# Attention summed by parts: value differences instead of weights, and future keys set to one on GpSimd

## The chip, the cores and the metric

The kernel runs on one core of a Trainium2 chip. The metric is the device time of one execution in microseconds (us); for the kernel before, three executions were timed, and one more was recorded by the profiler.

## The reference, cut to what matters

The program computes a state-space layer with an MLP, then a "stick-breaking" attention layer with an MLP, then a second block (a recurrent mixer, a sparse attention and a feed-forward part). Sequence length is 512, width 1024. Only the stick-breaking attention is touched: 16 heads of 64, for each query t and key s < t

```
z_ts   = q_t . k_s / 8
beta   = sigmoid(z),  keep = 1 - beta = sigmoid(-z)
o_t    = sum over s < t of  beta_ts * (product of keep_tj for s < j < t) * v_s
mix    = o @ w_o
```

Keys at or after the query take no part: their keep counts as 1 and their weight as 0. Let S_s be the product of keep_tj over j = s .. t-1. Then the weight of key s is S_(s+1) - S_s, and the same sum can be written over differences of neighbouring values, v_(s-1) - v_s, with S_s itself as the factor.

## The kernel before, in words

One core runs five instruction queues written out by hand: TensorE (products), ScalarE (activations and copies out of PSUM), VectorE, GpSimd (which splits each weight chunk into a high and a low part, `split_chunks`, lines 443 and 446), and SyncE (weight loads). They are tied by semaphores alone; the order in each queue is the order in the code. `build` lists the stages. At the end of some stages all four compute engines meet: each drains, counts `phase_done` up, and waits for the other three (line 3199). `sb_project` and `sb_attend` both end with such a meeting.

`sb_project` (line 1434) multiplies the 512 tokens by the query, key and value weights. TensorE takes weight chunks that GpSimd has split, up to six chunks ahead; ScalarE copies the results from PSUM: q and k as features by tokens (line 1450), v as tokens by features, `vTok` (line 1454), in eight pieces of 128 tokens by 512 features, the first four for heads 0 to 7. VectorE has nothing in this stage. GpSimd splits six chunks past the stage's own before it goes to the meeting.

`sb_attend` (line 1463) has 32 units: 8 pairs of heads by 4 blocks of 128 queries. The unit of block i has (i + 1) x 128 keys. The blocks of pair 0 come in the order 0, 1, 2, 3, those of the later pairs 3, 2, 1, 0; so "512-wide" is block 3 and "384-wide" block 2. For a unit u:

- TensorE makes the logits of both heads (line 1513), and adds a product of the identity with `past_mask`, which holds -1e30 for keys at or after the query, on the diagonal block of each head (line 1518).
- ScalarE makes keep = sigmoid(-z) (line 1560) and beta = sigmoid(z), called `weights` (line 1561). When the second is done, the logits' PSUM banks are free (`s_b`).
- VectorE turns keep into running products from the last key backwards with one scan for each head (line 1591), waits for them, and multiplies beta by the product of the key behind (line 1595).
- TensorE transposes the weights block by block (line 1529); ScalarE copies them out of PSUM (line 1568); TensorE multiplies them with `vTok` (line 1541).
- After the four units of a pair ScalarE takes the high part of the output (line 1572) and VectorE the low part (line 1599).

TensorE's order is logits(u+1), transposes(u-1), output(u-2). ScalarE's is the sigmoids of u, then the copy of u-2. VectorE's is the scans and the multiplication of u. Logits have two pairs of PSUM banks, keep and weights three buffers each, transposed weights one PSUM place and two buffers. GpSimd has no work in `sb_attend`.

Of the kernel before, what the change touches and what calls it, by code (L numbers as in the profile page):

```python
# [60 lines left out]
FAR = -1.0e30  # L61
# [423 lines left out]
class Norm:  # L485
# [948 lines left out]
def sb_project(nc, kit, m, a):  # L1434

    gq = Gemm(kit, a["sb_w_q"], KD, 0, D, True)
    gk = Gemm(kit, a["sb_w_k"], KD, 0, D, True)
    gv = Gemm(kit, a["sb_w_v"], KD, 0, D, False)
    before = kit.norm

    def tensor(pe):
        gq.tensor(pe, m.x_tile, norm=before)
        gk.tensor(pe, m.x_tile)
        gv.tensor(pe, m.x_tile)

    def scalar(act):
        for g, dst in ((gq, m.qF), (gk, m.kF)):
            for n in range(g.count):
                ps = g.wait_tile(act, n)
                act.activation(dst[:, n, :], ps, ACT.Copy, scale=HD ** -0.5 if g is gq else 1.0)\  # L1450
                   .then_inc(kit.tile_free, 1)
        for n in range(gv.count):
            ps = gv.wait_tile(act, n)
            act.activation(m.vTok[:, n % NT, (n // NT) * WIDE:(n // NT + 1) * WIDE], ps, ACT.Copy)\
               .then_inc(kit.tile_free, 1)

    def gpsimd(pool):
        kit.split_chunks(pool, gv.last_chunk + SPLIT)

    return tensor, None, scalar, gpsimd  # L1460


def sb_attend(nc, kit, m, a):

    s_mask = kit.sem("sb_mask_ready")
    s_z = kit.sem("sb_logits_ready")  # L1470
    s_k = kit.sem("sb_keep_ready")
    s_b = kit.sem("sb_break_ready")
    s_w = kit.sem("sb_weights_ready")
    s_t = kit.sem("sb_weights_transposed")
    s_c = kit.sem("sb_weights_copied")
# [24 lines left out]
    def weights(u):  # L1500
        return m.broken[:, u % 3, :, 0:width(u)]

    def turned(u):
        return m.wT[:, u % 2, :, 0:width(u)]

    def tensor(pe):
        def logits(u):
            p, i = UNITS[u]
            if u >= 2:

                pe.wait_ge(s_b, u - 1)
            for s in range(2):
                pe.matmul(logit_banks(u)[:, s], m.qF[rows(s), p, block(i)], m.kF[rows(s), p, 0:width(u)],  # L1513
                          start=True, stop=False, skip_group_check=True)
            if u == 0:
                pe.wait_ge(s_mask, 1)
            for s in range(2):
                mm = pe.matmul(logit_banks(u)[:, s, block(i)], m.ident_r, m.past_mask, start=False, stop=True,
                               skip_group_check=True)
            mm.then_inc(s_z, 1)  # L1520

        def turn(u):
            pe.wait_ge(s_w, u + 1)
            if u >= 1:

                pe.wait_ge(s_c, u)
            for s in range(2):
                for b in range(UNITS[u][1] + 1):
                    mm = pe.transpose(kit.psum[:, TURNED + s, block(b)], weights(u)[:, s, block(b)], m.ident[:, :])
            mm.then_inc(s_t, 1)  # L1530

        def out(u):
            p, i = UNITS[u]
            pe.wait_ge(s_c, u + 1)
            if p >= 2 and u % NT == 0:

                pe.wait_ge(s_of, p - 1)
            for b in range(i + 1):
                for s in range(2):
                    h = 2 * p + s  # L1540
                    mm = pe.matmul(kit.psum[rows(s), OUT + p % 2, block(i)], m.vTok[:, b, h * 64:(h + 1) * 64],  # L1541
                                   turned(u)[:, s, block(b)], start=(b == 0), stop=(b == i), skip_group_check=True)
            mm.then_inc(s_o, 1)

        logits(0)
        for u in range(U + 2):
            if u + 1 < U:
                logits(u + 1)
            if 1 <= u <= U:
                turn(u - 1)  # L1550
            if u >= 2:
                out(u - 2)

    def scalar(act):
        act.preload_act_table_set("sigmoid_and_others")

        def sigmoids(u):

            act.wait_ge(s_z, u + 1)
            act.activation(keep(u), logit_banks(u), ACT.Sigmoid, scale=-1.0).then_inc(s_k, 1)  # L1560
            act.activation(weights(u), logit_banks(u), ACT.Sigmoid).then_inc(s_b, 1)

        def copy(u):
            act.wait_ge(s_t, u + 1)
            if u >= 2:

                act.wait_ge(s_o, u - 1)
            act.activation(turned(u), kit.psum[:, TURNED:TURNED + 2, 0:width(u)], ACT.Copy).then_inc(s_c, 1)

        def high(p):  # L1570
            act.wait_ge(s_o, NT * (p + 1))
            act.activation(m.xin.high[:, p, :], kit.psum[:, OUT + p % 2, :], ACT.Copy).then_inc(s_oh, 1)

        for u in range(U + 3):
            if u < U:
                sigmoids(u)
            if 2 <= u < U + 2:
                copy(u - 2)
            if u >= 6 and u % NT == 2:
                high(u // NT - 1)  # L1580

    def vector(dve):
        step = kit.vector_chain(dve)

        def breaks(u):

            dve.wait_ge(s_k, u + 1)
            n = width(u)
            for s in range(2):
                x = keep(u)[:, s][:, ::-1]  # L1590
                step.mark(dve.tensor_tensor_scan(x, x, m.ones[:, 0:1].broadcast_to([P, n]), 1.0, ALU.mult, ALU.mult))  # L1591
            step.wait()
            dve.wait_ge(s_b, u + 1)
            w = weights(u)[:, :, 0:n - 1]
            dve.tensor_tensor(w, w, keep(u)[:, :, 1:n], ALU.mult).then_inc(s_w, 1)

        def low(p):
            dve.wait_ge(s_oh, p + 1)
            dve.tensor_tensor(m.xin.low[:, p, :], kit.psum[:, OUT + p % 2, :], m.xin.high[:, p, :].bitcast(F32),
                              ALU.subtract).then_inc(s_of, 1)  # L1600

        dve.tensor_scalar(m.past_mask, m.upper, FAR, None, ALU.mult).then_inc(s_mask, 1)
        for u in range(U + 4):
            if u < U:
                breaks(u)
            if u >= 7 and u % NT == 3:
                low(u // NT - 1)

    return tensor, vector, scalar, None


def head_sums(kit, m, pe, bank, t, squares):
# [1367 lines left out]
class Memory:  # L2980


    def __init__(self, kit):
# [46 lines left out]
        b, r, s = self.big, self.rows_mem, self.small  # L3030
# [23 lines left out]
        whole = kit.nc.alloc_sbuf_tensor_at("big_rounded", [P, BIG], F32R, offset=big_at)  # L3054
# [15 lines left out]
        self.keep, self.broken = self.part(b, 12288, 3, 2, SEQ), self.part(b, 15360, 3, 2, SEQ)  # L3070
        self.wT = self.part(b, 18432, 2, 2, SEQ)
        self.past_mask = whole[:, 20480:20480 + P]

        self.rwF = self.part(b, 0, RW_COLS // P, SEQ)
        self.qkTok = self.part(b, 3072, NT, 2 * ATT)
# [30 lines left out]
        w = self.spare  # L3106
# [43 lines left out]
def build(nc, a, out):  # L3150
    with ExitStack() as ctx:
# [134 lines left out]
```

## Time and profile before

| what | us |
|---|---|
| median of 3 runs | 2448.83 |
| lowest, highest | 2448.54, 2456.0 |
| profiled execution, its own time | 2456.86 |
| span in its trace (first to last instruction) | 2455.1 |
| busy: TensorE, VectorE, ScalarE, GpSimd | 2375.3, 1021.6, 609.9, 1458.5 |
| mean granted TensorE clock | 0.986 |

The profile has one execution. Busy time is the time in which an engine has an instruction in work; TensorE's instructions overlap, so a busy TensorE need not be at its peak. "Idle before" names the instruction that ended a wait. The chain of waits goes back from the last instruction to whatever released each step, so only what stands in it moves the end. Line numbers are those of the kernel before; L3199 is the meeting of the engines. The attention stage runs from about 967 to about 1057 us.

### The profile page before, as it was taken

To read this page: it belongs to the slowest core of one execution; us is meant where nothing else is said; L and a number is where in the kernel's file an instruction comes from. 1 tells how busy PE (TensorE), PEld (TensorE's weight loads), DVE (VectorE), ACT (ScalarE), POOL (GpSimd) and SP (SyncE) were. 2 spreads that over 40 slices of the span, in tenths; PEclk is the share of its full clock that TensorE was granted. 3 is DMA by queue.
4 is the path that set the end of the run, shared out by engine and by line. 5 is a ranking of instruction groups with operands and counts; after the bars stand their busy time and mean duration, and the time that the engine had idled before them with its cause. 6 is when DMAs were issued, how large, how long until landed. Compare 5 with 4: busy or idle time off the path is not lost.

```text
span 2455.1 us, 34580 instructions
## 1 busy us (share of the span) xinstructions
PE 2375.3 (97%) x14346; PEld 1935.6 (79%) x14346; DVE 1021.6 (42%) x1558; ACT 609.9 (25%) x1271; POOL 1458.5 (59%) x1260
## 2 busy tenths in 40 slices
PE   8999999999999999999999999999798999999998
PEld 6887778888888886678888877766686788888887
DVE  3547673551141502954305264885532325211114
ACT  2223663020010112721102022356442211110010
POOL 7665777586586665029759647650123766665863
PEclk9999999999999999999999999999898999999999
DMA  5331114232232232014323313120001332332321
GB/s 168 92 89 44 52 52 153 80 120 95 86 112 95 80 109 78 1 44 137 101 71 121 96 54 103 52 86 10 3 4 36 99 97 83 104 101 79 108 89 62
DMA packets 104432, 199.04 MB, mean 81 GB/s; under 512 B 9322, under 2 KB 12628, under 8 KB 104276
## 3 DMA queue, kind: packets, MB, share of 16 engines
q1 hardware_dynamic: 101620, 189.36, 24.9%
q10 hardware_dynamic: 2656, 7.47, 0.9%
q8 instruction: 113, 1.85, 0.3%
q14 instruction: 43, 0.35, 0.0%
HBM read 194.71 MB, written 2.10 MB: 80 GB/s over the span
## 4 chain that ended last, share of the span: by engine, by line
PE 73%; DVE 6%; POOL 3%; issue 1%; ACT 1%; DVEq 0%; POOLq 0%; ACTq 0%
PE psum L160 32%; PE psum L304 25%; PE psum L162 4%; PE psum L242 3%; POOL weight_split_ring L446 2%; DVE big L1591 1%; PE psum L204 1%; DVE big L2058 1%; POOL weight_split_ring L443 1%; PE psum L1513 1%; DVE best L2057 1%; PE psum L2370 0%; PE psum L1541 0%; PE psum L2299 0%; PE psum L2363 0%
## 5 line engine op out<-in xcount | busy, mean ns | idle before, releaser
L446 POOL TENSOR_TENSOR weight_split_ring<-weight_ring,weight_split_ring 128x512 fp32r<-128x512 f32 (+3 forms) x732 | 962.1, 1335 | 30.5
L160 PE MATMUL psum<-x_split,weight_split_ring 128*128 128x512 f32 x4128 | 970.7, 393 | 4.0 <-POOL weight_split_ring L446 2.4
L160 PEld LDWEIGHTS psum<-x_split,weight_split_ring 128*128 128x128 f32 x4128 | 766.4, 187 | 176.0 <-issue 10.5
L443 POOL TENSOR_SCALAR weight_split_ring<-weight_ring 128x1024 fp32r<-128x1024 f32 (+3 forms) x366 | 395.3, 1080 | 675.1 <-PE psum L304 369.8
L304 PE MATMUL psum<-weight_split_ring,hidden_split 128*128 128x512 f32 x2256 | 514.1, 389 | 0.0
L304 PEld LDWEIGHTS psum<-weight_split_ring,hidden_split 128*128 128x128 f32 x2256 | 423.0, 188 | 87.5
L162 PE MATMUL psum<-weight_split_ring,x_split 128*128 128x512 f32 x864 | 217.8, 400 | 0.3 <-ACT big L1872 0.3
L162 PEld LDWEIGHTS psum<-weight_split_ring,x_split 128*128 128x128 f32 x864 | 156.4, 188 | 37.8 <-issue 7.2
L762 DVE TENSOR_TENSOR big<-big 128x512 f32<-128x512 f32 x64 | 88.0, 1375 | 177.2 <-ACT big L747 177.2
L747 ACT ACTIVATE big<-psum 128x512 f32<-128x512 f32 x64 | 38.3, 599 | 429.7 <-PE psum L160 374.9
L545 DVE SCALAR_TENSOR_TENSOR residual<-residual,psum 128x512 f32<-128x512 f32 x48 | 32.7, 682 | 218.1 <-PE psum L304 217.9
L480 DVE SCALAR_TENSOR_TENSOR residual<-residual,psum 128x512 f32<-128x512 f32 x24 | 16.5, 687 | 204.6 <-PE psum L304 204.6
L242 PE MATMUL psum<-x_split,weight_split_ring 128*128 128x256 f32 x768 | 97.2, 287 | 4.5 <-DVE x_split L535 2.5
L242 PEld LDWEIGHTS psum<-x_split,weight_split_ring 128*128 128x128 f32 x768 | 94.7, 194 | 5.9 <-DVE x_split L535 3.3
L2957 DVE TENSOR_TENSOR big<-big,psum 128x512 f32<-128x512 f32 x22 | 15.1, 687 | 195.9 <-PE psum L160 195.9
L764 DVE TENSOR_TENSOR hidden_split<-big,hidden_split 128x512 fp32r<-128x512 f32 x64 | 94.1, 1470 | 2.2
L623 ACT ACTIVATE deviation<-mean_square 128x1 f32<-128x1 f32 x24 | 4.9, 203 | 335.9 <-DVE mean_square L556 335.9
L2602 POOL TENSOR_TENSOR big<-big,pair_masks 128x512 f32<-128x512 f32 x20 | 26.7, 1344 | 93.3 <-PE psum L2346 55.5
L304 PE MATMUL psum<-weight_split_ring,big_rounded 128*128 128x512 f32 x288 | 69.2, 395 | 0.1
L304 PE MATMUL psum<-weight_split_ring,x_split 128*128 128x512 f32 x288 | 67.5, 390 | 1.5 <-DVEq L3199 1.5
L304 PEld LDWEIGHTS psum<-weight_split_ring,x_split 128*128 128x128 f32 x288 | 53.8, 188 | 12.9 <-DVEq L3199 1.7
L304 PEld LDWEIGHTS psum<-weight_split_ring,big_rounded 128*128 128x128 f32 x288 | 53.5, 188 | 11.8 <-issue 0.2
(352 smaller groups left out, 2440.8 us busy)
## 6 DMA issues: line engine op xcount, KB each, us to landing
weight_ring<-in_mlp_w SPq DMA_DIRECT2D x128, 512.0 KB, 3.7
weight_ring<-in_w_in SPq DMA_DIRECT2D x92, 512.0 KB, 3.6
weight_ring<-in_w_ffn_in SPq DMA_DIRECT2D x40, 512.0 KB, 3.7
weight_ring<-in_w_out SPq DMA_DIRECT2D x24, 512.0 KB, 3.7
weight_ring<-in_w_ffn_out SPq DMA_DIRECT2D x22, 512.0 KB, 3.6
weight_ring<-in_sb_w_q SPq DMA_DIRECT2D x8, 512.0 KB, 3.8
weight_ring<-in_sb_w_k SPq DMA_DIRECT2D x8, 512.0 KB, 3.7
weight_ring<-in_sb_w_v SPq DMA_DIRECT2D x8, 512.0 KB, 3.6
```

The lines of the kernel that those rows point to most:

```text
L160: mm = pe.matmul(out, wp[:, k, m * P:m * P + rows], xp, start=first, stop=last)
L162: mm = pe.matmul(out, xp[:, m * P:(m + 1) * P], wp[:, k, 0:n], start=first, stop=last)
L204: mm = pe.matmul(out, xp[:, t * P:(t + 1) * P], wp[:, k, 0:n], start=b == 0 and k == 0 and q == 0, stop=b == last and k == nk - 1 and q == 2)
L242: mm = pe.matmul(out, wp[:, k, m * P:(m + 1) * P], xp[:, cols], start=first, stop=last, skip_group_check=True)
L304: mm = pe.matmul(out, xp[:, t * P:(t + 1) * P], wp[:, k, :], start=first and k == 0 and q == 0, stop=last and k == nk - 1 and q == 2)
L443: pool.tensor_scalar(part.high[:, 0:nk, 0:n], raw, 1.0, 0.0, ALU.mult, ALU.add).then_inc(self.high_made, 1)
L446: low = pool.tensor_tensor(part.low[:, k, 0:n], raw[:, k, :], part.high[:, k, 0:n].bitcast(F32), ALU.subtract)
L545: dve.scalar_tensor_tensor(out=hs, in0=hs, scalar=self.alpha, in1=ps, op0=ALU.mult, op1=ALU.add)\
L747: act.activation(m.relu_tmp[:, n % 2, :], ps, ACT.Relu).then_inc(kit.tile_free, 1)
L762: step(dve.tensor_tensor(sq, r, r, ALU.mult))
L764: dve.tensor_tensor(m.hid.low[:, n % HALF, :], sq, m.hid.high[:, n % HALF, :].bitcast(F32), ALU.subtract)\
L2602: pool.tensor_tensor(m.level[s], m.kb[s], across(m.pair_mask[:, 1 + lv, 0:64], HEADS), ALU.mult)\
```

## The change

The weights are no longer formed. keep is scanned as before, and the running products S themselves are transposed and multiplied by differences of values.

- The mask products, the second sigmoid and VectorE's multiplication go, and with them `weights` and its buffers. The logits' banks are free after the one sigmoid.
- A new GpSimd part in `sb_attend` waits for each unit's sigmoid and sets keep to 1 at and after the query, with one `affine_select` on the diagonal block of both heads (128 partitions by 2 x 128). VectorE's scans wait for it (`s_m`).
- In `sb_project` ScalarE's queue, after each copy of a value piece, also waits for its own copy and issues a DMA that writes the piece shifted by one token into `vStep` (partitions 1 to 127), and another for the row that crosses to the next block: 8 large copies and 6 single rows. VectorE sets one row to zero.
- `value_step` on VectorE, once for each of the eight pieces, subtracts: `vStep` becomes v_(s-1) - v_s; and `vTok` becomes the same, with v added again in its last row only. The first four run in `sb_project`, the other four in `sb_attend`, each behind the scans of units 4 to 7. The output products take `vTok` for the diagonal block and `vStep` for the others, and wait for the steps (`sb_steps`).
- `wT` moves to other memory.

```diff
@@ sb_project
+    def value_step(dve, n):
+        v, d = m.vTok[:, n % NT, cols(n)], m.vStep[:, n % NT, cols(n)]
+        dve.wait_ge(s_vs[n // NT], 16 * (2 * NT - 1))
+        kit.vector_chain(dve)(dve.tensor_tensor(d, d, v, ALU.subtract))
+        dve.scalar_tensor_tensor(out=v, in0=v, scalar=m.ident[:, P - 1:P], in1=d, op0=ALU.mult, op1=ALU.add)\
+           .then_inc(m.sb_steps, 1)
...
+            act.activation(m.vTok[:, b, cols(n)], ps, ACT.Copy).then_inc(kit.tile_free, 1)
+            gv.wait_free(act, n)
+            act.dma_start(m.vStep[1:P, b, cols(n)], m.vTok[0:P - 1, b, cols(n)]).then_inc(s_vs[n // NT], 16)
+            if b < NT - 1:
+                act.dma_start(m.vStep[0:1, b + 1, cols(n)], m.vTok[P - 1:P, b, cols(n)]).then_inc(s_vs[n // NT], 16)
+    def vector(dve):
+        kit.vector_chain(dve)(dve.memset(m.vStep[0:1, 0, :], 0.0))
+        for n in range(NT):
+            value_step(dve, n)
@@ sb_attend
-                pe.wait_ge(s_b, u - 1)
+                pe.wait_ge(s_k, u - 1)
             for s in range(2):
                 pe.matmul(logit_banks(u)[:, s], m.qF[rows(s), p, block(i)], m.kF[rows(s), p, 0:width(u)],
-                          start=True, stop=False, skip_group_check=True)
-            for s in range(2):
-                mm = pe.matmul(logit_banks(u)[:, s, block(i)], m.ident_r, m.past_mask, start=False, stop=True,
-                               skip_group_check=True)
-            mm.then_inc(s_z, 1)
+                          start=True, stop=True).then_inc(s_z, 1)
...
-                    mm = pe.transpose(kit.psum[:, TURNED + s, block(b)], weights(u)[:, s, block(b)], m.ident[:, :])
+                    mm = pe.transpose(kit.psum[:, TURNED + s, block(b)], keep(u)[:, s, block(b)], m.ident[:, :])
...
+            pe.wait_ge(m.sb_steps, NT if p < PAIRS // 2 else 2 * NT)
             for b in range(i + 1):
+                v = m.vTok if b == i else m.vStep
...
-            act.activation(weights(u), logit_banks(u), ACT.Sigmoid).then_inc(s_b, 1)
...
-            dve.wait_ge(s_k, u + 1)
+            dve.wait_ge(s_m, u + 1)
...
-            step.wait()
-            dve.wait_ge(s_b, u + 1)
-            w = weights(u)[:, :, 0:n - 1]
-            dve.tensor_tensor(w, w, keep(u)[:, :, 1:n], ALU.mult).then_inc(s_w, 1)
...
+            if NT <= u < 2 * NT:
+                m.sb_value_step(dve, u)
...
+    def gpsimd(pool):
+        for u in range(U):
+            pool.wait_ge(s_k, u + 1)
+            own = keep(u)[:, :, block(UNITS[u][1])]
+            pool.affine_select(out=own, in_=own, compare_op=ALU.is_gt, fill=1.0, base=0, pattern=[[0, 2], [-1, P]],
+                               channel_multiplier=1).then_inc(s_m, 1)
```

## Rows read from the trace of the kernel before

**Rows 1.** The page, busy us, share of the span, instructions.

```profile
PE 2375.3 (97%) x14346; PEld 1935.6 (79%) x14346; DVE 1021.6 (42%) x1558; ACT 609.9 (25%) x1271; POOL 1458.5 (59%) x1260
```

**Rows 2.** Chain of waits, one steady pair: start us, us, what.

```profile
1030.52 1.02 PE psum L1541 x16
1031.54 1.06 PE psum L1513 x4
1032.60 0.39 PE psum L1518 x2
...
1033.01 1.03 ACT big L1560
...
1035.21 1.21 DVE big L1591
...
1036.44 0.62 DVE big L1595
...
1037.58 1.81 DVE big L1591 x2
...
1039.41 0.97 DVE big L1595
...
1040.43 0.87 PE psum L1529 x6
```

**Rows 3.** Instructions by line, 966 to 1058: busy us, mean ns | idle before.

```profile
L1591 DVE TENSOR_TENSOR_SCAN big<-big,constants 128x128 f32<-128x128 f32 (+3 forms) x64 | 49.1, 809 | 8.8 <-ACT big L1560 8.7
L1595 DVE TENSOR_TENSOR big<-big 128x254 f32<-128x254 f32 (+3 forms) x32 | 26.4, 824 | 1.1
L1599 DVE TENSOR_TENSOR x_split<-psum,x_split 128x512 fp32r<-128x512 f32 x8 | 5.5, 685 | 1.8 <-ACT x_split L1572 1.8
...
L1518 PE MATMUL psum<-big_rounded,exact_identity 128*128 128x128 f32 x64 | 14.8, 315 | 0.0
```

**Rows 4.** Windows: length, busy PE, PEld, DVE, ACT, POOL; clock, DMA, GB/s.

```profile
968.00:976.00 8.00, 8.00 (x29) 3.70 (x25) 6.23 (x10) 4.85 (x9) 0.00 (x0) 0.50 0.17 59
...
988.00:1042.00 54.00, 50.37 (x426) 32.85 (x424) 48.24 (x64) 40.99 (x66) 0.00 (x0) 1.00 0.01 1
1730.00:1740.00 10.00, 6.64 (x107) 6.25 (x109) 4.17 (x8) 2.94 (x6) 1.12 (x3) 0.66 0.01 2
```

**Rows 5.** Timeline of TensorE, logits that open pairs 1 and 2.

```profile
976.00 1.92 PE L1513 MATMUL psum<-big 64*128 64x512 f32 x4
...
988.33 1.13 PE L1513 MATMUL psum<-big 64*128 64x512 f32 x4
```

**Rows 6.** Timeline of TensorE, first instructions of this and the next stage.

```profile
966.66 0.49 PE L1513 MATMUL psum<-big 64*128 64x128 f32 x4 [3.90 <-POOLq L3199]
...
1057.34 0.76 PEld L304 LDWEIGHTS psum<-weight_split_ring,x_split 128*128 128x128 f32 x4 [1.71 <-DVEq L3199]
```

**Rows 7.** Timeline of ScalarE and GpSimd before the attention stage.

```profile
962.79 0.60 ACT L1454 ACTIVATE big<-psum 128x512 f32<-128x512 f32 x1 [0.76 <-PE psum L162]
962.92 1.05 POOL L443 TENSOR_SCALAR weight_split_ring<-weight_ring 128x1024 fp32r<-128x1024 f32 x1 [1.76 <-PE psum L162]
964.05 2.48 POOL L446 TENSOR_TENSOR weight_split_ring<-weight_ring,weight_split_ring 128x512 fp32r<-128x512 f32 x2
```

**Rows 8.** Timeline of VectorE and GpSimd, selects alone and side by side.

```profile
1561.79 0.75 DVE L2043 SCALAR_TENSOR_TENSOR big<-big,index_weights 128x512 f32<-128x512 f32 x1
...
1562.69 0.29 POOL L2011 TENSOR_SCALAR_AFFINE_SELECT big<-big 128x128 f32<-128x128 f32 x1 [10.57 <-DVE big L2043]
...
1565.08 1.20 DVE L2028 TENSOR_TENSOR big<-big,heads_by_token 128x1024 f32<-128x1024 f32 x1
1565.08 1.72 POOL L709 TENSOR_SCALAR_AFFINE_SELECT pair_masks<-pair_masks 128x64 f32<-128x64 f32 x1
1566.21 1.25 DVE L2029 TENSOR_TENSOR big<-big,heads_by_token 128x1024 f32<-128x1024 f32 x1
```

**Rows 9.** Instructions by line, a 128x512 operation of VectorE beside GpSimd's splits.

```profile
L762 DVE TENSOR_TENSOR big<-big 128x512 f32<-128x512 f32 x64 | 88.0, 1375 | 177.2 <-ACT big L747 177.2
```

More of the change, by code:

```diff
@@ L1439, in sb_project, with cols @@
     before = kit.norm
+    s_vs = [kit.sem(f"sb_shifted_values_landed{n}") for n in range(2)]
+    m.sb_steps = kit.sem("sb_value_steps_ready")
+    def cols(n):
+        return slice(n // NT * WIDE, (n // NT + 1) * WIDE)
+    def value_step(dve, n):
[4 more added lines that the diff above has]
+           .then_inc(m.sb_steps, 1)
     def tensor(pe):
@@ L1453, in scalar @@
             ps = gv.wait_tile(act, n)
-            act.activation(m.vTok[:, n % NT, (n // NT) * WIDE:(n // NT + 1) * WIDE], ps, ACT.Copy)\
-               .then_inc(kit.tile_free, 1)
+            b = n % NT
+            act.activation(m.vTok[:, b, cols(n)], ps, ACT.Copy).then_inc(kit.tile_free, 1)
[7 more added lines that the diff above has]
+            value_step(dve, n)
     def gpsimd(pool):
         kit.split_chunks(pool, gv.last_chunk + SPLIT)
-    return tensor, None, scalar, gpsimd
+    m.sb_value_step = value_step
+    return tensor, vector, scalar, gpsimd
 def sb_attend(nc, kit, m, a):
-    s_mask = kit.sem("sb_mask_ready")
+    s_m = kit.sem("sb_keep_masked")
     s_z = kit.sem("sb_logits_ready")
     s_k = kit.sem("sb_keep_ready")
[L1472 to L1475, printed above, removed]
+    s_w = kit.sem("sb_survival_ready")
+    s_t = kit.sem("sb_survival_transposed")
+    s_c = kit.sem("sb_survival_copied")
     s_o = kit.sem("sb_out_ready")
@@ L1498, in keep @@
         return m.keep[:, u % 3, :, 0:width(u)]
-    def weights(u):
-        return m.broken[:, u % 3, :, 0:width(u)]
     def turned(u):
@@ L1509, in logits @@
             if u >= 2:
-                pe.wait_ge(s_b, u - 1)
+                pe.wait_ge(s_k, u - 1)
             for s in range(2):
                 pe.matmul(logit_banks(u)[:, s], m.qF[rows(s), p, block(i)], m.kF[rows(s), p, 0:width(u)],
-                          start=True, stop=False, skip_group_check=True)
-            if u == 0:
-                pe.wait_ge(s_mask, 1)
-            for s in range(2):
-                mm = pe.matmul(logit_banks(u)[:, s, block(i)], m.ident_r, m.past_mask, start=False, stop=True,
-                               skip_group_check=True)
-            mm.then_inc(s_z, 1)
+                          start=True, stop=True).then_inc(s_z, 1)
         def turn(u):
@@ L1537, in out @@
                 pe.wait_ge(s_of, p - 1)
+            pe.wait_ge(m.sb_steps, NT if p < PAIRS // 2 else 2 * NT)
             for b in range(i + 1):
+                v = m.vTok if b == i else m.vStep
                 for s in range(2):
                     h = 2 * p + s
-                    mm = pe.matmul(kit.psum[rows(s), OUT + p % 2, block(i)], m.vTok[:, b, h * 64:(h + 1) * 64],
+                    mm = pe.matmul(kit.psum[rows(s), OUT + p % 2, block(i)], v[:, b, h * 64:(h + 1) * 64],
                                    turned(u)[:, s, block(b)], start=(b == 0), stop=(b == i), skip_group_check=True)
@@ L1557, in sigmoids @@
         def sigmoids(u):
-            act.wait_ge(s_z, u + 1)
+            act.wait_ge(s_z, 2 * u + 2)
             act.activation(keep(u), logit_banks(u), ACT.Sigmoid, scale=-1.0).then_inc(s_k, 1)
-            act.activation(weights(u), logit_banks(u), ACT.Sigmoid).then_inc(s_b, 1)
         def copy(u):
@@ L1582, in vector, with survive @@
     def vector(dve):
-        step = kit.vector_chain(dve)
-        def breaks(u):
-            dve.wait_ge(s_k, u + 1)
+        def survive(u):
+            dve.wait_ge(s_m, u + 1)
             n = width(u)
@@ L1590, in breaks @@
                 x = keep(u)[:, s][:, ::-1]
-                step.mark(dve.tensor_tensor_scan(x, x, m.ones[:, 0:1].broadcast_to([P, n]), 1.0, ALU.mult, ALU.mult))
-            step.wait()
-            dve.wait_ge(s_b, u + 1)
-            w = weights(u)[:, :, 0:n - 1]
-            dve.tensor_tensor(w, w, keep(u)[:, :, 1:n], ALU.mult).then_inc(s_w, 1)
+                ins = dve.tensor_tensor_scan(x, x, m.ones[:, 0:1].broadcast_to([P, n]), 1.0, ALU.mult, ALU.mult)
+            ins.then_inc(s_w, 1)
         def low(p):
@@ L1600, in low @@
                               ALU.subtract).then_inc(s_of, 1)
-        dve.tensor_scalar(m.past_mask, m.upper, FAR, None, ALU.mult).then_inc(s_mask, 1)
         for u in range(U + 4):
             if u < U:
-                breaks(u)
+                survive(u)
+            if NT <= u < 2 * NT:
+                m.sb_value_step(dve, u)
             if u >= 7 and u % NT == 3:
                 low(u // NT - 1)
-    return tensor, vector, scalar, None
+    def gpsimd(pool):
[4 more added lines that the diff above has]
+                               channel_multiplier=1).then_inc(s_m, 1)
+    return tensor, vector, scalar, gpsimd
 def head_sums(kit, m, pe, bank, t, squares):
@@ L3069, in __init__ @@
         self.vTok = self.part(b, 8192, NT, D)
-        self.keep, self.broken = self.part(b, 12288, 3, 2, SEQ), self.part(b, 15360, 3, 2, SEQ)
-        self.wT = self.part(b, 18432, 2, 2, SEQ)
-        self.past_mask = whole[:, 20480:20480 + P]
+        self.keep = self.part(b, 12288, 3, 2, SEQ)
+        self.vStep = self.part(b, 16384, NT, D)
+        self.wT = self.part(r, 0, 2, 2, SEQ)
         self.rwF = self.part(b, 0, RW_COLS // P, SEQ)
```

## The prediction

> **What bounds the kernel now.** First the page's busy shares: TensorE is busy 97% of the span [rows 1], so a saving counts only where TensorE itself waits or does the removed work. The change touches two stages. The attention stage begins with the first logits at 966.66 us and ends with the next stage's first product at 1057.34 [rows 6]: 90.7 us. In the chain of waits one head pair repeats, from its 512-wide output product at 1030.52 to the next such product, which follows the transposes that end at 1041.30 (40.43 + 0.87): a period of 10.78 us [rows 2]. The reader should see that this is a loop through four engines, with no engine full. TensorE does output (1.02), logits (1.06) and mask (0.39). ScalarE makes the first sigmoid (1.03). VectorE does the two 512-wide scans (from the sigmoid's end, 34.04, until 35.21 + 1.21: some 2.35 and handoffs of 0.02), then the multiplication (0.62, and 0.52 more until the next scan starts at 37.58), two 384-wide scans (1.81) and their multiplication (0.97). TensorE transposes (0.87). By totals over 8 pairs, VectorE has 49.1 us of scans, 26.4 of multiplications and 5.5 of low parts, 10.1 us per pair [rows 3]. Inside the window of five steady pairs TensorE is busy 50.37 of 54 us [rows 4], but that counts overlapping latencies and filled waits.
>
> **Own time.** The profiled execution took 2456.86 us around a span of 2455.1. The three timed runs gave 2448.54, 2448.83 and 2456.0. So the profile's execution stands 8.0 us above the median. I work out a difference from its rows and take it from the median.
>
> **Part 1, the steady pair.** Going: the mask products, of which 0.39 is on the chain. Without them the logits' own tail shows, about 0.07 us (estimate: a 512-wide group lasts 1.13 in its row [rows 5], its pitch on the chain is 1.06). Going too: the second sigmoid, which is not on the chain, and the multiplications, 0.62 + 0.52 + 0.97 and two handoffs of 0.02. What remains is transposes 0.87, output 1.02, logits 1.13, sigmoid 1.03 with 0.02, scans 2.35 and 1.81 with 0.04 at the end: 8.27 us [rows 2]. Coming: a GpSimd select, in series between sigmoid and scan. Starting GpSimd on another engine's work costs some 0.15: L2043 on VectorE ends at 1562.54 and the select starts at 1562.69 [rows 8]. With 0.05 for the way back, 0.20. The select's length S: a 128x128 select takes 0.29 us [rows 8]. This one has 2x128 elements. I put S at 0.40 (estimate: 0.29 plus another 128 elements at the pace at which the 1024-element split on GpSimd runs, 1.05 us [rows 7]). Low end 0.29. The high end is the select that ran beside VectorE, 1.72 us for only 64 elements, of which 1.20 was waiting for VectorE's instruction at the same start [rows 8]; the rest is 0.52, so 0.6 bounds the work of 256.
>
> The unseen resource is what VectorE and GpSimd do to each other. The select that began with L2028 at 1565.08 ended at 1566.80, after L2028 ended at 1566.28 and while L2029 ran; L2029 lasted 1.25 against L2028's 1.20 [rows 8]. So GpSimd waits for the two-input instruction, then slips in before the next one is finished, and the next loses little. For 256 elements I take a hold of h = 0.20 on VectorE (estimate: four times the 0.05 that 64 elements cost L2029). Low end nothing; high end all of S. A select is issued while another unit's scans run, so about two holds fall between the scans of the chain, and the select's own S once. Pair = 8.27 + 0.20 + S + 2h = 9.27 us, 1.51 less than 10.78. VectorE then has 49.1/8 + 5.5/8 + 4 x 0.20 = 7.6 us of work in a pair, TensorE 50.37/5 - 14.8/8 = 8.2 [rows 3, 4]: neither full, so the loop still sets the pace.
>
> The Trainium skill ("SBUF — State Buffer", Who interferes with whom) states that a VectorE instruction with two SBUF inputs and a GpSimd instruction reading SBUF exclude each other, the first keeping the pair for its whole instruction. The first half the trace shows (0.52 after 1.20 of waiting); the second, that the next VectorE instruction would lose all of S, it doesn't show at L2029. By that rule h = S and it is the first rival below.
>
> **Part 2, value differences.** Four of the eight steps run on VectorE in the projection stage, beside TensorE's products. They cost nothing (the stage gives VectorE no other work); beside GpSimd's splits they may take the 1.38 us per instruction of L762 instead of the 0.68 of L1599, which has the same size [rows 3, 9]: 11 us in all. They can start when the first half of the value products is out, and the second half alone asks four splits of GpSimd, 4 x 3.6 us [rows 7]. The splits that they slow run up to six chunks ahead of TensorE. The boundary is set by GpSimd's last split, 964.05 to 966.53, while ScalarE's last copy ends at 963.39 [rows 7]. So ScalarE has 3.1 us for the waits and DMA issues now queued behind its copies (14 in all, three or fewer in that gap). If a copy is late there, the boundary moves by at most a DMA issue's few tenths. SBUF-to-SBUF copies do not occur in the trace. Their second half is needed by VectorE only after unit 4, 10 us past the boundary; later than that, every scan behind the first value step would wait the difference. I price it at nothing, and a few us at worst.
>
> The other four steps stand in VectorE's order behind units 4 to 7. Each is a subtraction and a dependent scale-and-add of 128x512, 0.68 each, 1.36 together, 5.4 in all. VectorE has 9.27 - 7.6 = 1.7 us spare in a pair. Pairs 1 and 2 together now take 12.33 + 10.78 = 23.1 us [rows 2, 5]. Bounds: 18.5 + 5.4 - 3.3 = 20.7 if the slack takes what it can, 24.0 if none. I take 23.5, because two steps lie right between the chain's scans: **+0.4**. What was gained in these pairs is spent on the value steps.
>
> **Part 3, both ends.** Pair 0 runs at a TensorE clock of 0.50 (1.2 GHz) [rows 4] after 3.90 us idle [rows 6]; nothing in the change alters that gap. From 966.66 to the logits of unit 4 at 976.00 it takes 9.34 us [rows 5, 6]. There the mask products run at half clock, four times some 0.7 (estimate: twice the chain's 0.39, less overlap); part hides behind the table load, and the select adds a little: **-1.8**. The last pair has the loop's gain of 1.5 and then a drain ruled by TensorE: **-1.3**. Pairs 3 to 6, four of them: 4 x -1.51 = **-6.1**.
>
> **Sum**: -1.8 + 0.4 - 6.1 - 1.3 = -8.8 us, stage 82 instead of 90.7, and 2448.83 - 8.8 = **2440.0 us**.
>
> **Rivals.**
> *A. Full lock.* h = S = 0.40: pair 9.67, four pairs -4.4, pairs 1 and 2 +1.3, ends -1.8 and -1.1: -6.0, time 2442.8. For it: the wait of 1.20 in rows 8. Against it: L2029's 1.25. Chance 0.20, with select lengths up to 0.6 (2447) in it.
> *B. The clock stays low, slower than before.* The stage begins at 0.50, and the mask products that helped keep TensorE full go away, while in pairs 1 and 2 it waits for the value steps. If it is still at 1.2 GHz there, a pair costs 2 x 8.2 = 16.4 us instead of 9.27, 7.1 more; three such pairs give +21 - 9 = +12, time 2461. It decides from 9/7.1, about 1.3 pairs, on. For it: the clock was 0.66 in 1730 to 1740, where TensorE was busy 6.64 of 10 us [rows 4]. Against it: 1.00 throughout the steady pairs [rows 4], whose waits on the scans stay of the same kind. Chance 0.08.
> *C. No interference.* h = 0, S = 0.29: pair 8.76, four pairs -8.1, pairs 1 and 2 -2.4, ends -3.5: -14, time 2434.8. For it: no scan in the trace runs beside GpSimd, so none shows a conflict. Chance 0.12.
> *D. The select replaces the wait.* A pair is 8.47 + S + 2h; with h = S it reaches 10.78 at S = 0.77, and with the value steps the stage is slower than before from about 0.7. At 0.9: pair 11.2, +1.6 for four, +3 in pairs 1 and 2: about +3, 2452. Against: the 0.29 rows. Chance 0.04.
> The forecast has the remaining 0.56.
>
> **Numbers.** A measurement here tells about 0.3%, 7.3 us, from no change, and the forecast of -8.8 lies just past it; the runs of one kernel themselves lie 7.4 us apart. The forecast and C give faster, unless the median falls on a long run (about one in four); A mostly falls within. Faster 0.53, same 0.36, slower 0.11. Range: from C, 2434.5, to the upper select with a long run, 2450.
>
> **What would show it.** Right: no L1518-like product, pair pitch in the chain 9.1 to 9.7, stage 80 to 84 us, selects of 0.4 us (more where they wait for a scan), pairs 1 and 2 about 11.7 each with the value steps in VectorE's chain, GpSimd on the chain between sigmoid and scan. Wrong: selects over 0.7 us, scans of 512 lengthened from 1.21 to 1.6, a granted clock of 0.50 beyond 980 us, or a boundary after the projection later than 966.6.

## The result and the profile after

The change made the kernel slower: 2497.46 us (median of 4 runs, 2490.95 to 2498.77) against 2452.41 (4 runs, 2448.54 to 2459.1), a ratio of 1.0176 with a 95% interval of 1.0159 to 1.0193. The prediction was 2440.0 us, in a range of 2434.5 to 2450.0.

The page of the changed kernel shows where it is. Each digit is the busy share, in tenths, of one of 40 equal slices of the span. TensorE has two neighbouring slices at 4 and 6 tenths, where before it had 9, and its granted clock falls in them.

```profile
span 2495.1 us, 34479 instructions
PE 2363.3 (95%) x14282; PEld 1926.6 (77%) x14282; DVE 1002.6 (40%) x1542; ACT 590.7 (24%) x1239; POOL 1477.2 (59%) x1292
PE   8999999999999994699999999999798999999998
PEclk9999999999999997799999999999898999999999
```

Against [rows 1] TensorE is busy 12 us less, in a span 40 us longer. Next the first products of the two stages, on TensorE's timeline of the changed kernel (start, length, what, and in brackets the idle time before and what ended it):

```profile
1015.51 3.40 PE L1533 MATMUL psum<-big 64*128 64x128 f32 x12 [51.46 <-ACTq L3217]
...
1100.40 9.82 PE L304 MATMUL psum<-weight_split_ring,x_split 128*128 128x512 f32 x42 [1.47 <-DVEq L3217]
```

These answer to [rows 6]; line numbers are those of the kernel that the rows come from, and L3217 is the meeting of the engines here. Before the stage TensorE idles 51.46 us instead of 3.90, and ScalarE's queue, not GpSimd's, comes last to the meeting: +47.6 us. The stage itself then takes 1100.40 - 1015.51 = 84.9 us instead of 90.7: -5.8. Together +41.8, of the span's +40.0; the rest lies outside the two stages.

What ScalarE's queue did is on its timeline (columns as above; ACTq are its DMA issues). L1468 is the copy of a value piece, L1471 the issue of its 127-row shift, L1473 that of the single row:

```profile
944.99 0.60 ACT L1468 ACTIVATE big<-psum 128x512 f32<-128x512 f32 x1 [6.15 <-issue]
945.62 0.65 ACTq L1471 DMA_DIRECT2D big<-big  x1
946.30 11.96 ACTq L1473 DMA_DIRECT2D big<-big  x1
...
958.31 0.60 ACT L1468 ACTIVATE big<-psum 128x512 f32<-128x512 f32 x1 [12.71 <-issue]
...
959.60 13.50 ACTq L1473 DMA_DIRECT2D big<-big  x1
```

The work of a piece is 0.6 us; a single DMA issue behind it holds the queue for up to 13.5. The single rows look guilty, since theirs are the long issues. The windows say otherwise (length, busy time of TensorE, its weight loads, VectorE, ScalarE, GpSimd; then clock, DMA share, GB/s). After the weights had landed, only the shifts moved:

```profile
978.00:980.00 2.00, 0.00 (x0) 0.00 (x0) 0.00 (x0) 0.00 (x0) 0.00 (x0) 0.50 0.07 26
```

A share of 0.07 of 16 engines is one engine, and it moves 26 GB/s. A shift of 127 rows of 2 KB is then 10 us. Every compute engine is idle, and TensorE's clock is at 0.50, 1.2 GHz.

In the steady part the change did what it was to do. The chain of waits of one pair (start, length, what; "issue" is time in which the engine waited for nothing that the profile shows; L1557 is the output product, L1533 the logits, L1576 the sigmoid, L1624 the select, L1604 the scans, L1543 the transposes, L1583 their copy):

```profile
1058.02 1.02 PE psum L1557 x16
1059.04 1.11 PE psum L1533 x4
...
1060.17 1.03 ACT big L1576
...
1061.34 0.42 POOL big L1624
...
1061.78 2.35 DVE big L1604 x2
...
1064.17 1.11 PE psum L1543 x8
1065.28 0.02 issue
1065.30 1.03 ACT gain_rows L1583
1066.34 0.14 issue
1066.47 0.85 PE psum L1543 x6
1067.32 1.02 PE psum L1557 x16
```

From 1058.02 to 1067.32 it is 9.30 us, against 10.78 in [rows 2]; the forecast was 9.27. But it is not the chain I had drawn. It doesn't go through the 384-wide scans; it goes from the 512-wide scans to their transposes (L1543 x8), ScalarE's copy of them (L1583), and only then to the 384-wide transposes.

### The profile page after: what moved, and what is told of

It is laid out like the page before. It is cut to its first block, busy times and chain, and to the rows that moved or that the text cites. A ratio compares the mean times of both kernels' runs of the same rounds, so it can differ in the third digit from the quotient of the medians.

```text
span 2495.1 us, 34479 instructions
## 1 busy us (share of the span) xinstructions
PE 2363.3 (95%) x14282; PEld 1926.6 (77%) x14282; DVE 1002.6 (40%) x1542; ACT 590.7 (24%) x1239; POOL 1477.2 (59%) x1292
## 4 chain that ended last, share of the span: by engine, by line
PE 71%; DVE 5%; POOL 3%; ACTq 3%; ACT 2%; issue 1%; DMA 1%; DVEq 0%; POOLq 0%
PE psum L160 31%; PE psum L304 24%; PE psum L242 3%; PE psum L162 2%; ACTq L1473 2%; POOL weight_split_ring L446 2%; PE psum L204 1%; DMA big<-big 1%; DVE big L2076 1%; PE psum L1543 1%; POOL weight_split_ring L443 1%; DVE big L1604 1%; PE psum L2388 1%; DVE best L2075 1%; ACTq L1471 1%
## 5 line engine op out<-in xcount | busy, mean ns | idle before, releaser
L162 PEld LDWEIGHTS psum<-weight_split_ring,x_split 128*128 128x128 f32 x864 | 156.5, 188 | 37.8 <-issue 7.2
L764 DVE TENSOR_TENSOR hidden_split<-big,hidden_split 128x512 fp32r<-128x512 f32 x64 | 87.0, 1359 | 2.2
L1624 POOL TENSOR_SCALAR_AFFINE_SELECT big<-big 128x256 f32<-128x256 f32 x32 | 18.8, 588 | 108.9 <-ACT big L1576 108.9
L1533 PE MATMUL psum<-big 64*128 64x128 f32 (+3 forms) x128 | 29.0, 537 | 51.6 <-ACTq L3217 51.5
```

Source lines behind the costliest of these rows:

```text
L162: mm = pe.matmul(out, xp[:, m * P:(m + 1) * P], wp[:, k, 0:n], start=first, stop=last)
L764: dve.tensor_tensor(m.hid.low[:, n % HALF, :], sq, m.hid.high[:, n % HALF, :].bitcast(F32), ALU.subtract)\
```

## The experiments

All kernels are cut from the changed one. The first four ask what holds ScalarE's queue, and what the value steps cost.

**126 + 1 rows.** Each 127-row copy becomes two.

```diff
-            act.dma_start(m.vStep[1:P, b, cols(n)], m.vTok[0:P - 1, b, cols(n)]).then_inc(s_vs[n // NT], 16)
+            act.dma_start(m.vStep[1:127, b, cols(n)], m.vTok[0:126, b, cols(n)]).then_inc(s_vs[n // NT], 16)
+            act.dma_start(m.vStep[127:P, b, cols(n)], m.vTok[126:P - 1, b, cols(n)]).then_inc(s_vs[n // NT], 16)
```

> The changed kernel with each shift copy of 127 rows cut into one of 126 rows and one of 1 row; same bytes, 22 DMAs instead of 14. Theory K (how many DMA engines a copy gets follows from its row count; 127 rows go through one engine at the 25 GB/s seen in the changed kernel, and ScalarE's queue stands behind them): the issues last under 1 us each, the boundary is back at about 966.6 us, the attention stage takes about 82 us, the whole about 0.35% less than before (2441 to 2445 against 2449). Rival Q (ScalarE's queue is held up by the number of DMA issues or by the single rows, whose issues took 4.8 to 13.5 us in the changed kernel): more issues, so no better or worse than the changed kernel, 2490 or more.

Measured: 2451.8 us (10 runs) against 2454.4 (14 runs), ratio 0.9989, interval 0.9979 to 0.9998; one row fewer in a DMA takes 45 us off the changed kernel. The copies are no longer slow either. In the trace of the value-step run below, which copies in the same way, there is a stretch in which only ScalarE's DMA queue moves data. The windows have length, clock, DMA share, GB/s:

```profile
942.25:942.50 0.25, 1.00 0.85 262
942.50:942.75 0.25, 1.00 0.91 295
```

That is some 14 engines of 16, and ten times 26 GB/s. ScalarE's timeline has no issue over 1.42 us left, here the last pieces:

```profile
964.86 0.81 ACTq L1471 DMA_DIRECT2D big<-big  x1
965.70 0.57 ACTq L1472 DMA_DIRECT2D big<-big  x1
966.30 0.61 ACTq L1474 DMA_DIRECT2D big<-big  x1
966.96 0.60 ACT L1468 ACTIVATE big<-psum 128x512 f32<-128x512 f32 x1 [2.13 <-issue]
...
969.49 0.80 PE L1534 MATMUL psum<-big 64*128 64x128 f32 x4 [6.67 <-ACTq L3218]
```

Theory K holds and Q falls, since there are 22 issues instead of 14. K missed the time, 0.11% under the kernel before instead of 0.35%, and the boundary: it is not back at 966.6. ScalarE still comes last, because three issues make a piece cost 2.7 us while TensorE makes one in 1.36 (the 0.76 idle and 0.60 busy of ScalarE's copy in [rows 7]). TensorE idles 6.67 us instead of 3.90. The stage takes from 969.49 to 1051.26, 81.8 us; 82 was forecast.

Pairs 1 and 2 hold something that the stage's length hides. TensorE waits there for VectorE, whose scans are held up by the value steps, as its timeline shows:

```profile
990.94 0.70 PE L1534 MATMUL psum<-big 64*128 64x256 f32 x4
993.99 1.97 PE L1544 MATMUL psum<-constants,big 128*128 128x128 f32 x8 [2.35 <-DVE big L1605]
```

Behind that wait TensorE's granted clock is back at 0.50, 1.2 GHz (windows with columns as above):

```profile
992.00:994.00 2.00, 0.01 (x1) 0.01 (x1) 2.00 (x3) 0.31 (x1) 0.41 (x1) 0.87 0.00 0
994.00:996.00 2.00, 2.00 (x10) 1.67 (x12) 2.00 (x3) 0.00 (x1) 0.00 (x0) 0.50 0.00 0
```

The same eight transposes take 1.09 us at full clock. From their start to the logits of the next pair it is 6.52 us here (993.99 to 1000.51), and 4.10 one pair later, where the clock is at 1.00 (1005.71 to 1009.81): the clock costs some 2.4 us.

**124 + 3 rows.** The same diff with 124.

> As the run with 126 rows, but cut into 124 and 3 rows. Theory K, as the Trainium skill has it (DMA: Bandwidth & Descriptors, section on why a DMA increments its semaphore by 16; the largest count up to 16 that divides the rows): 124 rows go over 4 engines, so a 248 KB copy takes about 2.5 us instead of 10, the row pace of the copies is 4 times that of 127 rows, and the stage starts within a few us of the run with 126 rows. A rival form of K (only a full 127 is bad, any cut spreads over all engines): the copies are as fast as with 126 rows. Rival Q: 2490 or more.

Measured: 2447.53 us, one run; the stage starts at 969.30, as with 126 rows, and takes 81.4 us. The number of engines shows in the windows. Late in the last shift, with nothing else under way, this kernel has a share of a quarter:

```profile
971.00:972.00 1.00, 0.50 0.26 96
972.00:973.00 1.00, 0.50 0.27 103
```

That is four engines of 16 and four times the changed kernel's 26 GB/s; the kernel with 126 rows has 0.01 and 0.00 in the same two windows, it is done. VectorE's first value step, which waits for the first half's shifts, starts at 957.41 here and at 950.82 with 126 rows. The copies are slower than over more engines, but fast enough not to hold the queue. The clock falls in pair 2 here as well, for a shorter time (0.55 and 0.60 from 996 to 1000 us), and pairs 1 and 2 take 23.5 us against 25.2 with 126 rows.

**No single rows.** The six copies between blocks are left out, the 127-row ones stay.

```diff
-            if b < NT - 1:
-                act.dma_start(m.vStep[0:1, b + 1, cols(n)], m.vTok[P - 1:P, b, cols(n)]).then_inc(s_vs[n // NT], 16)
```

> The changed kernel without the six single-row copies between blocks (those rows stay zero, so the values at block edges are left out). Theory K: the 127-row copies remain on one engine; the next issue then stands where the single rows stood, and the stage still starts late, at some 1000 to 1015 us, total about 2490. Rival Q with the single rows as the cause: the boundary is back at about 967, total about 2442.

Measured: 2496.15 us, one run. TensorE's first logits stand at 1013.24 behind 50.34 us of idleness, and the long issues are now those of L1471:

```profile
982.61 9.56 ACTq L1471 DMA_DIRECT2D big<-big  x1
...
992.85 9.56 ACTq L1471 DMA_DIRECT2D big<-big  x1
```

So the single rows were innocent. An issue that finds the queue full shows the time of the copies ahead of it, and 9.56 us of issue and the 0.6 us of ScalarE's copy are the 10 us of one shift.

**One value step a pair.** With the 126-row copies:

```diff
-            if NT <= u < 2 * NT:
-                m.sb_value_step(dve, u)
+            if u % NT == 3 and u < 4 * NT:
+                m.sb_value_step(dve, NT + u // NT)
```

> The 126-row version with the four value steps of the attention stage moved behind the one-block (or first four-block) unit that ends pairs 0 to 3, one a pair, instead of behind units 4 to 7. My theory: with two steps between the scans of a pair's wide units they cost about 4 us in pairs 1 and 2; one a pair in VectorE's slack of 1.7 us costs nearly nothing, so 3 to 4 us less than with units 4 to 7 (0.15%). Rival: VectorE is not on the chain in pairs 1 and 2 (the chain of the changed kernel goes through the copy of the transposes), and it makes no difference.

Measured: 2444.26 us (5 runs), ratio 0.9959, interval 0.9945 to 0.9974. The intervals of this and the 126-row version don't meet. In the traces the stage takes 1050.82 - 972.37 = 78.5 us, 3.3 less. The theory holds, the rival falls. The clock stays at 1.00 in pairs 1 and 2, which take 20.7 us instead of 25.2, 4.5 less; pair 0 takes 7.1 instead of 5.8. The medians differ by 7.5 us, more than the stage explains.

**Gathered single rows.** Only one DMA beside each copy, and two more at the end of each half:

```diff
+            act.dma_start(m.vStep[1:P - 1, b, cols(n)], m.vTok[0:P - 2, b, cols(n)]).then_inc(s_vs[n // NT], 16)
+            if b == NT - 1:
+                act.dma_start(m.vStep[P - 1:P, :, cols(n)], m.vTok[P - 2:P - 1, :, cols(n)]).then_inc(s_vs[n // NT], 16)
+                act.dma_start(m.vStep[0:1, 1:NT, cols(n)], m.vTok[P - 1:P, 0:NT - 1, cols(n)]).then_inc(s_vs[n // NT], 16)
```

> The spread version with the single rows of the four blocks of a half gathered in two DMAs at its end: 12 DMAs instead of 22, and only one beside each copy. In the two runs before, a piece cost ScalarE 0.61 + 0.81 + 0.57 + 0.61 us and some waits, 2.7 us, against TensorE's 1.36 us a piece, so the stage began 6.66 us after the last product instead of 3.90. Theory (the issue time on ScalarE's queue now sets the boundary): a piece costs about 1.45 us, the last one 0.6 + 0.8 + 0.6 + 0.6, the boundary falls back to GpSimd's last split, idle 3.9 to 4.2 us, total 2.5 us less than the spread version, ratio to before about 0.995. Rival (the boundary waits for the copies' data, not their issues): still 6 us or more.

Measured: 2442.06 us (6 runs) against 2455.57, ratio 0.9946, interval 0.9929 to 0.9963. The wait before the stage is back to what it was, on GpSimd:

```profile
966.91 3.36 PE L1534 MATMUL psum<-big 64*128 64x128 f32 x12 [3.90 <-POOLq L3218]
```

The boundary waited for issues and not for data, as the theory has it. The data of the last copies was still moving when the stage began. The stage takes 78.4 us instead of 90.7, 12.3 less, and the timed ratio gives 13. This version beats both kernels.

**No value steps in the attention stage.** The merged version without steps 4 to 7 (heads 8 to 15 are then summed over wrong differences).

> The merged version without the four value steps in the attention stage (heads 8 to 15 get wrong values; four subtractions and four scale-and-adds left out). Theory: once spread one a pair, the steps lie almost in VectorE's slack, so the stage here is at most 1 us shorter than in the merged, spread version (78 us). Rival: they still stand on the chain of pairs 0 to 2, and leaving them out gives 2 us or more.

Measured: 2439.9 us, one run. The stage takes 1044.61 - 966.49 = 78.1 us against 1045.29 - 966.91 = 78.4. Spread one a pair, the four steps cost 0.3 us of the stage. The theory holds. Pairs 1 and 2, from the logits of unit 4 to those of unit 12, take 19.8 us here (974.11 to 993.87), 20.6 when spread (974.00 to 994.55), and 25.2 with all four behind units 4 to 7 (975.30 to 1000.51 in the 126-row version).

**Two selects.** Each select of the merged version is issued again behind itself, and the scans wait for the second.

```diff
+            pool.affine_select(...).then_inc(s_m, 1)
+            pool.wait_ge(s_m, 2 * u + 1)
             pool.affine_select(...).then_inc(s_m, 1)
```

> The merged, spread version with every select issued twice, one after the other. In the changed kernel a steady pair takes 9.30 us on a chain of 512-wide transposes, their copy, 384-wide transposes, output, logits, sigmoid, select (0.42, with 0.13 ahead), two 512-wide scans. Theory from that chain: one select a pair is on it, so a pair grows by 0.42 plus some 0.1 for the wait between them, to 9.8 us. My forecast's chain (the select once plus two holds of VectorE): it grows by about 1.0 to 1.3, to 10.3 or more.

Measured: 2444.53 us, one run. A pair takes 10.14 us (996.39 to 1006.52), +0.84: between the two expectations, and neither chain is right. The loop has moved to the 384-wide unit:

```profile
1009.97 0.82 ACT big L1577
...
1010.92 0.42 POOL big L1625
...
1011.47 1.14 POOL big L1628
...
1012.63 2.15 DVE big L1605 x2
...
1014.83 0.88 PE psum L1544 x6
```

The second select of that unit takes 1.14 us instead of 0.42, beside scans of VectorE that run until 1012.40, and the two scans behind it 2.15 instead of 1.81. Those scans start at 1012.63, just after another select:

```profile
1012.56 0.40 POOL L1625 TENSOR_SCALAR_AFFINE_SELECT big<-big 128x256 f32<-128x256 f32 x1
1012.63 1.13 DVE L1605 TENSOR_TENSOR_SCAN big<-big,constants 128x384 f32<-128x384 f32 x1 [0.23 <-POOL big L1628]
```

They lose 0.34 us together; 0.33 us of that select were left when they started, and a third one starts beside them at 1013.10, so how the loss divides isn't shown. So the two engines do hold each other up, both ways. In the changed kernel this is small where it counts. Its rows by form (busy us, mean ns, idle before):

```profile
L1604 DVE TENSOR_TENSOR_SCAN big<-big,constants 128x512 f32<-128x512 f32 x16 | 18.9, 1225 | 12.1 <-POOL big L1624 12.1
L1624 POOL TENSOR_SCALAR_AFFINE_SELECT big<-big 128x256 f32<-128x256 f32 x32 | 18.8, 588 | 108.9 <-ACT big L1576 108.9
L1604 DVE TENSOR_TENSOR_SCAN big<-big,constants 128x384 f32<-128x384 f32 x16 | 15.4, 1005 | 1.8 <-POOL big L1624 1.8
```

A select alone is 0.42 us in the chain, on average 0.59: GpSimd waits. Of the scans, the 384-wide ones take 1005 ns instead of 941 in the kernel before, the 512-wide ones 1225 instead of 1212. All 64 scans together take 50.4 us instead of the 49.1 of [rows 3], so a select costs VectorE 0.04 us on average.

**The mask product again.** Merged and spread, selects replaced by the old products (the semaphores that go with them are left out of the diff).

```diff
-                          start=True, stop=True).then_inc(s_z, 1)
+                          start=True, stop=False, skip_group_check=True)
+            for s in range(2):
+                mm = pe.matmul(logit_banks(u)[:, s, block(i)], m.ident_r, m.past_mask, start=False, stop=True,
+                               skip_group_check=True)
+            mm.then_inc(s_z, 1)
```

> The merged, spread version with the old mask products on TensorE in place of the GpSimd selects: only the summation by parts of the change. The chain loses the select, 0.42 + 0.15, and gets the mask, 0.39 less the 0.07 of tail that it hides, so if the same chain holds a pair takes about 9.0 to 9.1 us instead of 9.3, 1 to 2 us less in all. Rival: TensorE, whose work grows by four mask products of 0.37 to about 9.5 us a pair, becomes the bound: 9.5 or more a pair, 1.5 us more in all.

Measured: 2445.85 us (8 runs), ratio 0.9965, interval 0.9948 to 0.9982. A pair takes 9.71 us (997.20 to 1006.91), and the whole chain of a pair is TensorE's, without a gap above 0.05:

```profile
by line: PE psum L1534 31.3%; PE psum L1564 29.6%; PE psum L1550 24.8%; PE psum L1539 14.8%; issue 0.6%
```

The rival holds. The summation by parts alone brings a pair from 10.78 to 9.71, and TensorE is then the bound; the select takes work off it and brings the pair to 9.30. In the timed runs that difference isn't clear: the interval overlaps that of the merged version, 0.9929 to 0.9963.

**113 + 14 rows.** To tell "the full 127 is bad" from the rule by divisors; the diff of the first run with 113.

> The changed kernel with each 127-row copy cut into 113 and 14 rows. The rule as the Trainium skill has it (DMA: Bandwidth & Descriptors, the engine count is the largest up to 16 that divides the rows) gives 113, a prime, one engine: 226 KB at the 25 GB/s of the changed kernel are 9 us a copy, 72 us for eight, so the stage starts at about 1000 to 1015 us and the total is 2480 or more. The other form (the full 127 is what is bad, any cut frees it) gives a start at about 969 us and 2447, as with 126 and 124 rows.

Measured: 2491.61 us, one run; TensorE idles 52.03 us and starts at 1014.58. The issue behind the 113-row copy again carries its time:

```profile
978.34 0.64 ACTq L1471 DMA_DIRECT2D big<-big  x1
979.01 7.53 ACTq L1472 DMA_DIRECT2D big<-big  x1
```

With nothing else under way the DMA share is 0.07 and 26 GB/s move, as with 127. Fewer rows than 124, and slow again: 126 and 124 rows are fast, 127 and 113, both primes, are slow. The largest divisors up to 16 are 14, 4, 1 and 1, and the shares of 0.85 to 0.91, 0.26, 0.07 and 0.07 are those of 14, 4, 1 and 1 engines of 16.

**Mask for the 512-wide units only.** Merged and spread; TensorE masks block 3, GpSimd selects for the others.

```diff
+            if i == NT - 1:
+                for s in range(2):
+                    mm = pe.matmul(logit_banks(u)[:, s, block(i)], m.ident_r, m.past_mask, start=False, stop=True,
+                                   skip_group_check=True)
...
+            if UNITS[u][1] == NT - 1:
+                continue
             pool.wait_ge(s_k, u + 1)
```

> The merged, spread version with the mask product on TensorE for the 512-wide units alone and the select for the other three of each pair. The steady chain of the merged version passes through the 512-wide unit's select only, 0.42 + 0.15; the mask costs that unit 0.39 less the 0.07 it hides, so the chain gives 9.05 us a pair, while TensorE's own work is 9.71 (all four masked) less 3 x 0.37, 8.6. Theory: 9.0 to 9.1 us a pair instead of 9.30, 1.5 us less in all. Rival: the loop closes through another unit (the 384-wide one, with its select, or VectorE held by selects), and the pair stays at 9.2 or more.

Measured: 2442.07 us (5 runs) against 2455.09, ratio 0.9949, interval 0.9934 to 0.9964, no different from the merged version's. A pair takes 9.23 us (1006.27 to 1015.50). The rival's number is right, and its reason isn't: no select and no scan is left on the chain. TensorE's own work, about 8.0 us of the pair, with one copy of ScalarE took their place:

```profile
1020.70 1.04 PE psum L1552 x8
...
1021.76 1.03 ACT gain_rows L1592
1022.80 0.14 issue
1022.93 0.85 PE psum L1552 x6
```

## Why the prediction was wrong

**The step that failed** is the one in part 2 on the boundary and the copies: that ScalarE's 3.1 us covered "the waits and DMA issues now queued behind its copies", that the boundary would move "by at most a DMA issue's few tenths", and that the copies' landing was priced "at nothing, and a few us at worst". It measured +47.6 us before the stage. I priced the issues, not what an issue does when the copies ahead of it have not drained, and I gave the copies no pace of their own, without asking how many DMA engines carry one. The runs show both. 127 rows go through one engine, at 26 GB/s and 10 us a copy, and eight of them stand in the queue that must reach the meeting. A cut to 126 and 1 rows, nothing else, removes it. The Trainium skill ("DMA: Bandwidth & Descriptors", the section on why a DMA increments its semaphore by 16 and not by 1) gives the rule, with 127 partitions as its example of a copy on one engine: the count is the largest up to 16 that divides the slowest dimension of both sides. The runs agree: one engine for 127 and 113 rows, four for 124, some 14 for 126. The prediction did not draw on it.

**The late landing**, named there as a wait of VectorE behind unit 4 and left at nothing, came too. In the changed kernel the last shift is issued at 1014.31 and VectorE's unit-4 step waits until 1032.79:

```profile
1014.31 18.46 DMA big<-big
...
1032.79 0.70 DVE big L1450
```

Pairs 1 and 2 take 27.2 us there (1022.50 to 1049.67) and 25.2 in the 126-row version: some 2 us.

**The value steps beside the projection** cost nothing at the boundary, as forecast. In the merged version they take up to 1.79 us an instruction beside GpSimd's splits, and two splits 3.30 us instead of 2.53, and still the stage begins 3.90 us after the last product.

**Part 1 was right in size, and partly by luck.** 9.30 against 9.27 us a pair. The select's S is 0.42 (0.40 assumed), the start of GpSimd and the way back 0.15 (0.20 assumed). The two holds of 0.20 that I added aren't on the chain, nor are the 384-wide scans; in their place stand the 512-wide transposes and their copy. What I had too much, 1.81 + 0.40, is 2.21 us; what I had left out is 1.11 + 0.02 + 1.03 + 0.14 = 2.30. That they match is luck. I followed the old chain and crossed out what went, and did not ask which other loop was nearly as long. The run with two selects shows what such a chain is worth: it grew by neither amount foreseen. Rival D (S above 0.77) falls. Rival A's hold comes into sight only with two selects, where a pair of scans loses 0.34 us, most of a select; in the changed kernel a select costs VectorE 0.04 us on average, nearer to C's nothing than to the 0.20 of the forecast. A's and C's pairs of 9.67 and 8.76 us did not come, since no hold stood on the chain and S was 0.42.

**Pairs 1 and 2** were forecast at 23.5 us, with 24.0 as the most. With data in time they take 25.2 (126 rows) and 23.5 (124 rows), and 19.8 without the steps. The bound of 24.0 had two steady pairs, 18.5 us, under the steps; pair 1 is longer than a steady pair, as it was before (12.33 against 10.78), and the two take 19.8. In the 126-row version the steps add 5.4 us, the sum of their lengths, but that is no sign that nothing hid in the slack. Some 2.4 us of it are the fallen clock, so the steps themselves cost some 3 (an estimate from the rows above). In the prediction's terms, the wait on VectorE was foreseen, and what it does to the clock was priced only in rival B. One a pair, the steps cost 0.3 us in the stage, and the clock stays up.

**The ends.** Pair 0 was forecast at 9.34 - 1.8; the merged version takes 974.00 - 966.91 = 7.1, close. The 126-row version takes 975.30 - 969.49 = 5.8, because its clock came back earlier: it is at 0.99 from 973 to 974 us. The 124-row version started at nearly the same time, is still at 0.50 there, and takes 7.1. The stage as a whole, with the copies repaired and the value steps where the change put them, is 81.8 us for a forecast of 82. That agreement is partly luck: the low side (pair 0) paid for the high one (pairs 1 and 2).

**Rival B** happened in part, and I had given it 0.08. Once the copies are repaired the clock is at 1.00 between 980 and 990 us in every trace, so it doesn't stay low. But where two value steps stand in the way of the scans, TensorE waits for VectorE and the clock falls again, as B has it: to 0.50 for some 6 us in the 126-row version, and after a wait of 5.06 us in the changed kernel (0.50 from 1038 to 1042). It cost some 2.4 us in the former, far from B's +21. The 0.50 before the stage in the changed kernel follows from the idleness, and doesn't cause it.

**Open.** The repaired stage and its boundary account for 8.9 - 2.8 = 6.1 us less than before in the traces; the timed ratio of the 126-row version gives 2.7 us, at most 5.1 by its interval. From there to the version with a step a pair it is the other way round, 3.3 us in the stage and 7.5 between the medians. Over both together the traces give 9.4 us and the timed ratio 10. Single executions of one kernel differ by up to 12 us in these runs (2448.53 to 2460.72 for the kernel before). The mean granted clock goes with it, 0.989 in the shortest and 0.983 in the longest; which comes first, and at what place of the kernel, no run here shows.

## What to carry to other kernels

Before a copy between partitions goes into a queue that a meeting or a barrier waits for, work out how many DMA engines its row count gives it, and take that pace times the number of copies as the time the queue may stand; choose 126 or 124 rows and a remainder instead of 127, and gather the remainders, since each issue takes its own 0.6 us. When an issue shows as long in a trace, look at the copy ahead of it, not at the one being issued. And when a step leaves a chain, look for the loop that is next in length; work dropped into an engine's slack is free only if it is spread as the slack is. Where it makes TensorE wait, look at the granted clock behind the wait as well.

## What the runs showed of the hardware

- A DMA of 127 or 113 rows moved 25 to 26 GB/s at a DMA share of 0.06 to 0.07; one of 124 rows 96 to 103 GB/s at 0.26 to 0.27; one of 126 rows 262 to 295 GB/s at 0.85 to 0.91. All have rows of 2 KB.
- An issue on ScalarE's queue takes 0.56 to 0.88 us when the queue takes it at once, the first of a kernel's value copies 1.21 to 1.43 us, and 6.8 to 13.6 us behind the later copies on one engine. Behind the first 127-row copy the next issue stood 4.82 us, behind the second 11.96.
- A select of 128x256 on GpSimd takes 0.42 us alone and up to 1.42 us beside VectorE's scans. Two 384-wide scans with one select just ahead and one beside them grew from 1.81 to 2.15 us.
- TensorE's granted clock fell to 0.50 after a wait of 2.35 us between busy stretches (126 rows), and did not come down in the traces with one value step a pair.
